# Two-layer encoder on one core: query strip between the gate products, forgetting weights normalized by GpSimd, values projected in a pair's own first steps

## The reference

```python
def mixer_sb_fox(x, w_in, b_f, w_o):
    h = x @ w_in                      # queries, keys, values of 8 + 8 heads of 64, and 8 gates
    ...
    f_logit = parts[6] + b_f
    oa = stick_breaking_attention(qa, ka, va)
    ob = forgetting_attention(qb, kb, vb, f_logit)
    return jnp.concatenate([oa, ob], axis=-1) @ w_o
```

## Time and profile before

| | us |
|---|---|
| median of 3 runs | 2926.17 (2924.12 to 2926.76) |
| profiled execution, its own time | 2929.35 |
| its span | 2927.6 |
| first score product of pair 0 | at 58.58 |
| pair 2 (stick-breaking) | 60.4 |
| pairs 4, 5, 6 (forgetting) | 63.6, 62.2, 63.9 |
| pair 7, to its last mask product | 42.8 |

### The profile page before, as it was taken

The page is one execution under the profiler, slowest core; times in us unless marked ns, Lnnn a source line. Parts: engine busy times, 40 slices in busy tenths (PEclk is TensorE's granted clock), DMA queues, the critical chain, the costliest instruction groups (busy, mean ns, idle before and its releaser), DMA issues.

```text
span 2927.6 us, 44713 instructions
## 1 busy us (share of the span) xinstructions
PE 2808.6 (96%) x16880; PEld 1461.5 (50%) x16880; DVE 1889.4 (65%) x2732; ACT 1089.5 (37%) x1797; POOL 1650.7 (56%) x883
## 2 busy tenths in 40 slices
PE   7999998899999999999999999999999999999998
PEld 3566655444444444454444444677764444444443
DVE  5777656386566664444999999677756756665042
ACT  3556666413333310013554333666641333332000
POOL 4677322365666669854438777600016566665884
PEclk9999999999999999999999999999999999999999
DMA  4122231431111144322113222211113211113422
GB/s 145 48 62 69 59 80 29 146 108 68 58 58 58 58 151 144 101 88 76 51 36 142 109 79 93 73 58 43 57 65 109 87 58 58 58 58 115 134 97 101
DMA packets 102989, 240.56 MB, mean 82 GB/s; under 512 B 42448, under 2 KB 42576, under 8 KB 102848
## 3 DMA queue, kind: packets, MB, share of 16 engines
q1 hardware_dynamic: 56352, 204.13, 20.1%
q10 hardware_dynamic: 46496, 34.48, 4.5%
HBM read 185.31 MB, written 31.51 MB: 74 GB/s over the span
## 4 chain that ended last, share of the span: by engine, by line
PE 83%; DVE 6%; ACT 3%; POOL 3%; issue 3%; ACTq 2%; DMA 0%; POOLq 0%; DVEq 0%
PE ps L1413 22%; PE ps L303 18%; PE ps L292 13%; PE ps L2220 6%; PE ps L553 5%; PE ps L327 3%; PE ps L2256 2%; PE ps L559 2%; PE ps L663 2%; PE ps L1740 2%; PE ps L748 2%; PE ps L1784 1%; PE ps L2235 1%; POOL w_hi L262 1%; PE ps L725 1%
## 5 line engine op out<-in xcount | busy, mean ns | idle before, releaser
L262 POOL TENSOR_TENSOR w_hi<-w_stage,ones 128x1024 bf16<-128x1024 f32 x147 | 307.9, 2094 | 341.3 <-PE ps L303 230.2
L265 POOL TENSOR_TENSOR w_lo<-w_stage,w_hi 128x1024 bf16<-128x1024 f32 x147 | 340.9, 2319 | 11.5
L1240 DVE SCALAR_TENSOR_TENSOR x_res<-x_res,ps 128x1024 f32<-128x1024 f32 x32 | 38.9, 1217 | 342.9 <-PE ps L303 342.9
L303 PE MATMUL ps<-w_hi,hid_hi 128*128 128x512 bf16 x704 | 209.5, 379 | 5.0 <-DVE x_res L1240 4.1
L303 PE MATMUL ps<-w_hi,hid_lo 128*128 128x512 bf16 x704 | 209.4, 379 | 0.0
L303 PE MATMUL ps<-w_lo,hid_hi 128*128 128x512 bf16 x704 | 209.2, 379 | 0.0
L2220 PE MATMUL ps<-lat_hi,q_now 128*128 128x512 bf16 (+3 forms) x768 | 197.7, 326 | 0.0
L1202 ACT ACTIVATE ln_rstd<-ln_rstd 128x1 f32<-128x1 f32 x32 | 6.5, 203 | 512.5 <-DVE ln_rstd L1249 512.5
L292 PE MATMUL ps<-xt_hi,w_hi 128*128 128x512 bf16 x608 | 180.8, 379 | 2.5 <-DVE score L1899 2.5
L292 PE MATMUL ps<-xt_lo,w_hi 128*128 128x512 bf16 x608 | 180.9, 379 | 0.0
L292 PE MATMUL ps<-xt_hi,w_lo 128*128 128x512 bf16 x608 | 180.8, 379 | 0.0
(11 more groups left out here) (291 smaller groups left out, 7776.6 us busy)
## 6 DMA issues: line engine op xcount, KB each, us to landing
w_stage<-in_l_up SPq DMA_DIRECT2D x88, 512.0 KB, 3.3
w_stage<-in_l_down SPq DMA_DIRECT2D x88, 512.0 KB, 3.3
w_stage<-in_l_o SPq DMA_DIRECT2D x32, 512.0 KB, 3.7
w_stage<-in_l_q SPq DMA_DIRECT2D x32, 512.0 KB, 5.2
q_split<-q_out SPq DMA_DIRECT2D x32, 512.0 KB, 2.6
q_now<-q_split SPq DMA_DIRECT2D x16, 1024.0 KB, 4.9
w_stage<-in_l_qkv SPq DMA_DIRECT2D x24, 512.0 KB, 3.3
x_spilled<-x_res ACTq DMA_DIRECT2D x16, 512.0 KB, 2.6
```

Source lines behind the costliest of these rows:

```text
L262: pool.tensor_tensor(w_hi[slot][:, 0:cols], w_stage[slot][:, 0:cols], ones[:, 0:1].to_broadcast([P, cols]), ALU.mult).then_inc(w_cast[slot ...
L265: pool.tensor_tensor(w_lo[slot][:, 0:cols], w_stage[slot][:, 0:cols], w_hi[slot][:, 0:cols], ALU.subtract).then_inc(w_split[slot], 1)
L303: mm = pe.matmul(ps[:, bank + h, :], a[:, k, rows], w[slot][:, h * HALF:(h + 1) * HALF], start=(k == 0 and m == 0), stop=(k == tiles - 1 a ...
```

## The change

There are three parts.

1. In the opening the DMA of the first weight strip goes ahead of most of xt, and PE projects both query halves of pair 0 piece by piece behind each gate product; the gate's signal is given before the last piece of these.
2. `half_slots` is turned: values are projected by the pair itself in its steps 0 to 3, queries and keys of the next pair in steps 4 to 12. Steps 13 to 15 have none. The copies of head 0's queries and keys move from step 11 to 14, those of the values to steps 5 and 6, and POOL's splits by one or two steps.
3. In the forgetting pairs POOL multiplies the weights by the inverse, and its splits stand between these products.

```diff
         def start_sync(sp):
-            for k in range(0, KT, 2):
+            sp.dma_start(xt_f[:, 0, :], t_in["xt"][:, 0, :]).then_inc(s_xt[0], 16)
+            load_piece(sp, feed_qkv, 0, 0)
+            for k in range(2, KT, 2):
                 sp.dma_start(xt_f[:, k, :], t_in["xt"][:, k, :]).then_inc(s_xt[k], 16)
-            load_first(sp, feed_qkv)
+            for n in (1, 2):
+                load_piece(sp, feed_qkv, n, 0)
...
-            mm.then_inc(s_gmm, 1)
+                if k == KT - 1:
+                    mm.then_inc(s_gmm, 1)
+                for e in range(2):
+                    proj_half(pe, e, 0, [k])
...
-        half_slots = [(0, 1), (2, 3, 4), (5, 6, 7), (8, 9), (10, 11, 12), (13, 14, 15)]
+        half_slots = [(4, 5), (6, 7), (8, 9, 10), (11, 12), (0, 1), (2, 3)]
...
+        def proj_pair(e, pair):
+
+            return pair if e >= 4 else pair + 1
...
-                if kind and prev:
-                    if slot == 0:
-                        make_current_qk(act, 1, pair)
-                    elif slot == 1:
-                        make_current_v(act, 0, pair)
-                    elif slot == 6:
-                        make_current_v(act, 1, pair)
-                if project and slot == 11:
+                if kind and prev and slot == 0:
+                    make_current_qk(act, 1, pair)
+                if kind and slot in (5, 6):
+                    make_current_v(act, slot - 5, pair)
+                if project and slot == 14:
                     make_current_qk(act, 0, pair + 1)
                 if kind == "fox" and slot == 0:
                     load_cum(act, 1, pair)
-                if project and slot == 11 and (kind == "fox" or isinstance(pair, int) and pair == N_SB // 2 - 1):
+                if project and slot == 14 and (kind == "fox" or isinstance(pair, int) and pair == N_SB // 2 - 1):
...
-                two_back, p2, t2 = trailing(pair, slot, kind, prev, 2)
-                n2 = (query_block(t2) + 1) * P
-                if two_back == "fox":
-
-                    w = prob[t2 % 4][:, 0:n2]
-                    act.wait_ge(s_ri, STEPS * (p2 - N_SB // 2) + t2 + 1)
-                    act.activation(w, w, ACT.Copy, scale=row_inv[:, t2 % 4:t2 % 4 + 1]).then_inc(s_wfox, 1)
...
+        def pair_gpsimd_fox(pool, pair, splits):
+
+            own = pair - N_SB // 2
+            for t in range(STEPS):
+                n = (query_block(t) + 1) * P
+                w = prob[t % 4][:, 0:n]
+                pool.wait_ge(s_ri, STEPS * own + t + 1)
+                pool.tensor_tensor(w, w, row_inv[:, t % 4:t % 4 + 1].to_broadcast([P, n]), ALU.mult).then_inc(s_wfox, 1)
+                splits(t)
...
+            def splits_ahead(pair):
+                def splits(t):
+                    if t == 3:
+                        split_qkv_hi(pool, 2, pair + 1)
+                    elif t == 4:
+                        split_qkv_lo(pool, 2, pair + 1)
+                    elif t in (8, 12):
+                        split_qkv_hi(pool, t // 12, pair + 2)
+                    elif t in (9, 13):
+                        split_qkv_lo(pool, t // 13, pair + 2)
+                return splits
...
+            def splits_o(t):
+                if t == 4:
+                    pool.wait_ge(s_pj, 6 * N_PAIRS)
+                if t in (4, 6, 8):
+                    split_first(pool, feed_o0, (t // 2 - 2,))
...
         def heads_tensor(pe):
-            for e in range(6):
+            for e in range(2, 4):
                 proj_half(pe, e, 0, range(8))
...
-            for e in range(4, 6):
-                proj_evac_hi(act, e, 0)
-            for hh in range(2):
-                make_current_v(act, hh, 0)
```

More of the change, by code:

```diff
@@ L529, in program @@
         s_half = sem("halves_set")
-        half_slots = [(0, 1), (2, 3, 4), (5, 6, 7), (8, 9), (10, 11, 12), (13, 14, 15)]
+        half_slots = [(4, 5), (6, 7), (8, 9, 10), (11, 12), (0, 1), (2, 3)]
         def proj_bank(e, pair):
-            return 2 + e if isinstance(pair, int) and pair == 0 else 4
+            return 2 + e if isinstance(pair, int) and pair == 0 and e < 4 else 4
         def proj_half(pe, e, pair, units):
             n, bank = e // 2, proj_bank(e, pair)
-            first = isinstance(pair, int) and pair == 0
+            first = isinstance(pair, int) and pair == 0 and e < 4
             for u in units:
@@ L567, in opens_half, with proj_slot, proj_ends @@
             return any(slots[0] == slot for slots in half_slots)
-        def proj_slot(pe, slot, pair):
+        def proj_pair(e, pair):
+            return pair if e >= 4 else pair + 1
+        def proj_slot(pe, slot, pair, project):
             for e, slots in enumerate(half_slots):
-                if slot in slots:
+                if slot in slots and (project or e >= 4):
                     at, of = slots.index(slot), len(slots)
[L573 to L579, removed]
+                    proj_half(pe, e, proj_pair(e, pair), range((8 * at + of - 1) // of, (8 * at + 8 + of - 1) // of))
+        def proj_ends(slot, pair, project):
+            return [(e, proj_pair(e, pair)) for e, slots in enumerate(half_slots)
+                    if (project or e >= 4) and slots[-1] + 1 == slot]
         def proj_dst(e, pair):
@@ L729, in pair_tensor @@
                     mm.then_inc(s_qk, 1)
-                    if project and not opens_half(slot):
-                        proj_slot(pe, slot, pair + 1)
+                    if not opens_half(slot):
+                        proj_slot(pe, slot, pair, project)
                 for part, cuts in enumerate((((0, 3), (0, 1)), ((3, TB), (1, TB // 2)))):
@@ L756, in pair_tensor @@
                 if prev is None and kind_then and t == 0:
-                    pe.wait_ge(s_pjl, 6)
+                    pe.wait_ge(s_pjl, 4)
                 if kind_then == "sb":
@@ L761, in pair_tensor @@
                     turning.turn(pe, p, t, s_wfox, STEPS * (p - N_SB // 2) + t + 1)
-                if kind and project and opens_half(slot):
-                    proj_slot(pe, slot, pair + 1)
+                if kind and opens_half(slot):
+                    proj_slot(pe, slot, pair, project)
         def mix_views(group, pair):
@@ L775, in pair_scalar @@
                 t, n = slot, (query_block(slot) + 1) * P
-                for e, p in proj_ends(slot, pair, project, prev is None) if kind else ():
+                for e, p in proj_ends(slot, pair, project) if kind else ():
                     proj_evac_hi(act, e, p)
@@ L861, in pair_vector @@
                     dve.wait_ge(s_sfree, STEPS * p1 + t1 + 1)
+                    wait_if(dve, s_wfox, STEPS * (p1 - N_SB // 2) + t1 - 3)
                     dve.reciprocal(row_inv[:, t1 % 4:t1 % 4 + 1], row_sum[:, t1 % 4:t1 % 4 + 1]).then_inc(s_ri, 1)
@@ L963, in heads_gpsimd, with splits_last @@
                 pair_gpsimd_sb(pool, pair)
-            with pool.Fori(N_SB // 2, N_PAIRS - 2) as pair:
[L965 to L974, removed]
+            def splits_ahead(pair):
+                def splits(t):
+                    if t == 3:
+                        split_qkv_hi(pool, 2, pair + 1)
+                    elif t == 4:
+                        split_qkv_lo(pool, 2, pair + 1)
+                    elif t in (8, 12):
+                        split_qkv_hi(pool, t // 12, pair + 2)
+                    elif t in (9, 13):
+                        split_qkv_lo(pool, t // 13, pair + 2)
+                return splits
+            def splits_last(t):
+                if t == 3:
+                    split_qkv_hi(pool, 2, N_PAIRS - 1)
+                elif t == 4:
+                    split_qkv_lo(pool, 2, N_PAIRS - 1)
+                elif t == 7:
+                    split_first(pool, feed_o0, (3,))
+            def splits_o(t):
[3 more added lines that the diff above has]
+                    split_first(pool, feed_o0, (t // 2 - 2,))
+            with pool.Fori(N_SB // 2, N_PAIRS - 2) as pair:
+                pair_gpsimd_fox(pool, pair, splits_ahead(pair))
+            pair_gpsimd_fox(pool, N_PAIRS - 2, splits_last)
+            pair_gpsimd_fox(pool, N_PAIRS - 1, splits_o)
         def heads_tensor(pe):
-            for e in range(6):
+            for e in range(2, 4):
                 proj_half(pe, e, 0, range(8))
@@ L1000, in heads_vector @@
         def heads_vector(dve):
-            for e in range(6):
+            for e in range(4):
                 proj_evac_lo(dve, e, 0)
```

6 lines of the change are left out of this document (removed).

## The result

| | before | changed |
|---|---|---|
| median, four runs each | 2926.47 us (2924.12 to 2930.02) | 2981.44 us (2981.03 to 2983.05) |
| ratio, 95% interval | | 1.0189 (1.0176 to 1.0201) |
| profiled execution, own time and span | 2929.35, 2927.6 | 2983.05, 2981.3 |

The forecast was 2953 us, its range 2922 to 2972. The sign came true; the time lies above the range.

What follows compares the result with a forecast made beforehand. PE, busy 96% of the span, was taken as the bound. The terms 14.4 + 2.8 + 8.4 - 1 + 2 = +26.6 us on 2929.35 gave 2956, as a median 2953 us, range 2922 to 2972.

Steps and rivals of the forecast that it cites:

- opening, to the first mask of pair 0: Before pair 0's first scores: earlier query split, values' projection gone, gate_x near 33; together -1 us (bounds -7 and +3).
- 14.4 + 4.8: Stick-breaking pair ends 0 to 3: +3.6 us each, +14.4 together, plus the clock's 1.2 us per end.
- 2.8 + 3.6: Three forgetting pair ends: +0.9 us each, +2.8 together, plus the clock's 1.2 us per end.
- The second path: Pair end, work queued behind the copies' DMAs on ACT: stay, take, pt_hi, then pt_lo, turn, scores; L = 9.2 us.
- L: Time from step 13's mask to the next pair's step 0 mask: 9.2 us, in forgetting pairs 9.6.
- other waits: PE's waits in a pair outside L, at steps 4 and 6: 1.5 us stick-breaking, 1.0 forgetting (bounds 0 and 3).
- The relief: ACT loses 12.4 us of normalizing per forgetting pair to POOL; taken as worth what the 1.0 us of waits allows.
- The clock: PE at half speed behind the waits at seven pair ends: 1.2 us each (between 0 and 3.4), +8.4 us.
- the clock falls at every end: Rival: every pair end costs the whole 3.4 us of lower clock, +42 us, 2968 us; chance 0.10.
- I let 6 us be hidden: Pair 7, steps 0 to 3: of 10.9 us added value projection 6 hidden, +5; relief gives back 3; +2 us.
- the 26.7 that I took: POOL's sixteen normalizing products in a forgetting pair: 26.7 us, from the row of its stick-breaking products; upper bound twice that.
- The rival that had POOL bound pair 7 at +8 us or more: Rival: POOL's products and weight splits in pair 7 give a late turn, +8 to +30, about 2965 us; chance 0.06.

Runs made afterwards that it cites:

- The run with SP's copies: The changed kernel with head 0's six query and key copies issued by SP, not ACT (gates' copy stays on ACT): 2962.43 us, 1.0122.
- the one with the late keys: The changed kernel with head 0's copies on SP, and the last key half over steps 11, 12 and 13, its split one step later: 2969.56 us, 1.0138.
- the filled wait: The changed kernel with 14 unused products ahead of the last turn at each of seven pair ends: 2969.48 us, 1.0143.
- those two kernels: Both with parts 1 and 3 and both heads' copies on SP: turned `half_slots` (2959.46 us, 1.0109) and old `half_slots` (2909.84 us, 0.9940).

## Why the forecast had the sign and not the size

The forecast's sum was +26.6 us on the profiled execution; measured were 2981.3 - 2927.6 = 53.7.

| | forecast | measured | off by |
|---|---|---|---|
| opening, to the first mask of pair 0 | -1 | -0.7 | +0.3 |
| pairs 0 to 3, clock included | 14.4 + 4.8 | +21.4 | +2.2 |
| pairs 4 to 6, clock included | 2.8 + 3.6 | +22.9 | +16.5 |
| pair 7 | +2 | +6.8 | +4.8 |
| all that follows | 0 | +3.3 | +3.3 |

- **The mechanism at the end of a pair was right.** The second path counted, step by step. From the mask of step 13 in pair 2: DMAs 2.0 us later (forecast 1.9), the stay 5.95 (5.7), stay, take and pt_hi up to the pt_lo 1.2 (1.4), the last turn 0.75 on (0.65). Up to there 7.9 us, forecast 7.8. The turn and the scores then took 2.6 us where 1.4 was written, at half clock. L is 10.5 where 9.2 was forecast. The run with SP's copies showed that the hold is part of it, and the one with the late keys that the landing was only next. The small miss of pairs 0 to 3 is partly luck: pairs 1 to 3 lost 20.7 us where 14.4 were forecast, and pair 0 only 0.7 where 4.8 were. Before the change pair 0 had waits of 1.19, 1.96 and 2.63 us in its steps 0 to 5, which became 0.71 and 0.74 us; the forecast had not looked at them.
- **The step that failed is the size of "other waits" in the forgetting pairs**: "1.0 in a forgetting one". Outside L pair 5 has three, 1.19, 1.34 and 2.18 us at steps 4, 6 and 11, 4.7 together, of the one kind named above. Each stands at a step that opens a half and so turns ahead of its projection:

```profile
415.56 1.14 PE L672 MATMUL ps<-ident,prob 128*128 128x128 f32 x7 [1.19 <-DVE pt_lo L693]
...
425.20 0.77 PE L672 MATMUL ps<-ident,prob 128*128 128x128 f32 x5 [1.34 <-DVE pt_lo L693]
...
446.06 0.66 PE L672 MATMUL ps<-ident,prob 128*128 128x128 f32 x4 [2.18 <-DVE pt_lo L693]
```

The forecast named steps 4 and 6; the largest wait stands at step 11, which it did not name. The pt_lo that ends it is small, but on DVE it comes behind the lo part of the key half that ended in step 10 and behind the next row maximum:

```profile
444.16 0.69 DVE L613 TENSOR_TENSOR nk_lo<-ps,nk_hi 128x512 bf16<-128x512 f32 x1 [0.39 <-ACT nk_hi L608]
444.77 0.81 DVE L837 TENSOR_REDUCE row_max<-ps 128x1 f32<-128x640 f32 x1
...
445.72 0.29 DVE L693 TENSOR_TENSOR pt_lo<-ps,pt_hi 128x128 bf16<-128x128 f32 x1
```

The row of before had two such steps with large turns, and I let the relief of ACT take off what the new order adds. The three waits are the same, to 0.01 us, with SP's copies, so the hold at step 14 has no part in them. L was also 2.1 us longer than the 9.6 of the forecast (11.57, 11.76 and 11.77 us in pairs 4 to 6). Its parts by the timeline of pair 5: 2.9 us to the first DMA, since the turn of step 13 waited 0.82 itself, 4.4 for the seven issues, then as in pair 2. Together 3.7 + 2.1 = 5.8 us a pair, which covers the 16.5 us (5.5 a pair).
- **The relief** was assumed to be worth what those waits left. It was worth 7 us alone (2920.40 against 2927.69 on the same chip) and nothing beside part 2 (1.0189 with it and without it). Less work in ACT's queue does not shorten the issue that the queue stands behind.
- **The clock**: 1.2 us an end was taken, 1.7 measured by the filled wait. The rival *the clock falls at every end* was half right. It did fall at every end, as the rule of the Trainium skill named in the prediction says (TensorE: Matmul & The Clock Gate, section "HAM oscillation — how this bites in real kernels"), though here the wait is for pt_lo and not for a DMA. The price was half of 3.4: the slow stretches at the seven ends are 44 us together, PE is busy 31 of them, and full speed could take off at most half of that, 16 us.
- **Pair 7**: "I let 6 us be hidden" failed. Of the 10.9 us of projection only 4.1 did not lengthen the pair, the relief of ACT included: PE is busy 38.36 us instead of 29.23 (9.1 more, at a clock of 0.95 instead of 0.91) and idle 11.3 instead of 13.6, so 2.3 us went into idle time. The 3 us of relief came to 0.7 (50.4 with ACT normalizing, 49.7 with POOL).
- **POOL**: 73.3 us in four pairs, 18.3 a pair against the 26.7 that I took. From 60 to 590 us the waits show PE waiting once for one of these products, in step 12 of pair 7. The rival that had POOL bound pair 7 at +8 us or more has this 2.1 us for it and no more:

```profile
PE ps L672 <- POOL prob L907: 2.1, 1, 2.1
```

- **The opening** came out near the forecast, -0.7 against -1, with gate_x at 31.50 (forecast 33). PE then waits 13.86 us for the copies, and by itself this part moved nothing.
- What the 3.3 us behind pair 7 are stays open. The change without part 3 does not have them (2391.4 us from the last mask of pair 7 to the end, as before the change, against 2394.7), and single executions of the kernel before lie up to 5.9 us apart. Nor did a run split the 50 us that part 2 costs without ACT's issues. By the traces of those two kernels 38 of them lie in pairs 0 to 6 and 7.5 in pair 7 (49.7 against 42.2 us). PE waits 63.7 - 57.7 = 6.0 us in pair 2 and 65.6 - 56.9 = 8.7 in pair 5 with the new order, 59.1 - 56.5 = 2.6 and 58.8 - 56.6 = 2.2 with the old one. That these are turns with no projection over them is read from the traces; only for one such wait, the 0.82 us of step 13, does a run show that projection takes it away.

## What to carry to other kernels

In this kernel a DMA issued from ACT's queue held everything behind it for the issue, 0.6 us each: look at what stands behind it, not only at when the copy must land, and put it on a queue that computes nothing. Projection work that looks movable was the cover of a chain over three engines (turn, pt_hi, pt_lo); before moving such filler, count each place where the chain is then bare, and price each at a full wait. A forecast that rests on one critical place needs the small waits counted too: in pair 5 five of 0.8 to 2.2 us made 6.9, the long one 4.0.

## What the runs showed of the hardware that was not expected

- Six DMA issues held ACT 3.9 us, and moving them to SP was worth 19 us in all, over seven pair ends, with landing times unchanged (2.2 to 2.4 us).
- POOL's product with a broadcast column as its second operand took 1147 ns in the mean over 64 (sixteen widths four times); its product of two full operands of the same widths took 1671 ns in the earlier trace rows and 1498 in the changed kernel. The two stand in different pairs, beside different work of DVE, so it is not shown that the operand makes the difference:

```profile
L888 POOL TENSOR_TENSOR prob<-take,prob 128x1024 f32<-128x1024 f32 (+3 forms) x64 | 95.7, 1498 | 124.1 <-DVE prob L867 124.1
```

- Fourteen products that do nothing useful, put into a wait, made the kernel 12 us faster: in pair 2 the granted clock stayed at 1.00, though the turn behind the wait began no earlier.
